# Forgetting attention: probabilities times values for two heads in one step, with the matmuls alternating between the two column halves of the TensorE array

## What is computed

```python
H_ATT = 16; HEAD_DIM = 64; Q_BLOCK = 128; s = 256

def forgetting_attention(q, k, v, f_logit):
    ...
    cum = jnp.cumsum(jax.nn.log_sigmoid(f_logit.astype(jnp.float32)), axis=1).transpose(0, 2, 1)
    for blk in range(s // Q_BLOCK):
        qs, qe = blk * Q_BLOCK, (blk + 1) * Q_BLOCK
        sc = jnp.einsum("bhqd,bhkd->bhqk", q[:, :, qs:qe], k[:, :, :qe]).astype(jnp.float32) * scale
        sc = sc + cum[:, :, qs:qe, None] - cum[:, :, None, :qe]
        ...
        p = jax.nn.softmax(sc, axis=-1).astype(v.dtype)
        outs.append(jnp.einsum("bhqk,bhkd->bhqd", p, v[:, :, :qe]))
```

## Time and profile before

| | us |
|---|---|
| median of 3 runs | 1188.36 (1187.55 to 1188.62) |
| the profiled execution | 1188.64 |
| its span, first to last instruction | 1186.8 |
| TensorE matmuls busy | 1161.3 (98% of the span) |
| TensorE weight loads busy | 1089.4 (92%) |
| DVE busy | 908.3 (77%) |
| ACT busy | 713.8 (60%) |
| POOL busy | 383.9 (32%) |

### The profile page before, as it was taken

How to read it: one execution, slowest core, us unless ns; L and a number is a source line. 1 busy time by engine, 2 the same in 40 slices (tenths; PEclk the granted TensorE clock), 3 DMA queues, 4 the chain that set the end, 5 groups by cost and what they waited for, 6 DMA issues and landing times.

```text
span 1186.8 us, 23771 instructions
## 1 busy us (share of the span) xinstructions
PE 1161.3 (98%) x8406; PEld 1089.4 (92%) x8406; DVE 908.3 (77%) x1365; ACT 713.8 (60%) x1142; POOL 383.9 (32%) x406
## 2 busy tenths in 40 slices
PE   8999999999999999998999999999999999999996
PEld 8999989999999999888999988888899999888886
DVE  7867897877699999557899698777666768877754
ACT  6498655654467676435745766665445546666552
POOL 3444000700545555224000135445220006554431
PEclk9999999999999999999999999999999999999999
DMA  6566433376635666652634356666765435665661
GB/s 216 178 195 212 143 111 121 124 255 191 207 107 178 184 186 180 212 187 77 182 126 146 100 168 203 181 191 205 253 198 178 144 124 176 197 187 183 210 201 69
DMA packets 56562, 204.32 MB, mean 172 GB/s; under 512 B 6688, under 2 KB 6840, under 8 KB 56368
## 3 DMA queue, kind: packets, MB, share of 16 engines
q1 hardware_dynamic: 54288, 197.35, 53.1%
q0 software_dynamic: 1632, 5.00, 1.2%
q10 hardware_dynamic: 576, 1.05, 0.2%
HBM read 202.29 MB, written 2.63 MB: 173 GB/s over the span
## 4 chain that ended last, share of the span: by engine, by line
PE 87%; DVE 9%; ACT 2%; issue 1%; DMA 1%; POOL 0%; DVEq 0%; SPq 0%; ACTq 0%; POOLq 0%
PE bank L1450 20%; PE bank L1456 14%; PE bank L1458 14%; PE bank L1457 14%; PE bank L1451 11%; DVE w_lo L734 2%; PE bank L1453 2%; PE bank L1560 2%; PE bank L1561 2%; PE bank L1562 2%; DVE h_two L764 1%; PE bank L1647 1%; DVE work L889 1%; DVE work L788 1%; PE bank L1637 1%
## 5 line engine op out<-in xcount | busy, mean ns | idle before, releaser
L734 DVE TENSOR_TENSOR w_lo<-raw,w_hi 128x1024 fp32r<-128x1024 f32 x374 | 477.4, 1284 | 133.2 <-ACT w_hi L310 128.8
L310 ACT ACTIVATE w_hi<-raw 128x1024 fp32r<-128x1024 f32 x374 | 391.6, 1052 | 133.6 <-PE bank L1458 62.5
L1456 PE MATMUL bank<-h_two,w_hi 128*128 128x256 f32 x1184 | 342.4, 289 | 11.3 <-DVE h_two L764 7.5
L1458 PE MATMUL bank<-h_two,w_lo 128*128 128x256 f32 x1184 | 335.6, 283 | 0.0
L1457 PE MATMUL bank<-h_two,w_hi 128*128 128x256 f32 x1184 | 335.6, 283 | 0.0
L1456 PEld LDWEIGHTS bank<-h_two,w_hi 128*128 128x128 f32 x1184 | 227.6, 192 | 17.9 <-issue 8.4
L1457 PEld LDWEIGHTS bank<-h_two,w_hi 128*128 128x128 f32 x1184 | 227.7, 192 | 0.3
L1458 PEld LDWEIGHTS bank<-h_two,w_lo 128*128 128x128 f32 x1184 | 227.6, 192 | 0.0
L1450 PE MATMUL bank<-h_two,w_hi 128*128 128x512 f32 x616 | 221.5, 398 | 0.9 <-DVE h_two L764 0.9
L1451 PE MATMUL bank<-h_two,w_lo 128*128 128x256 f32 x704 | 183.6, 281 | 0.0
L1450 PE MATMUL bank<-u_two,w_hi 128*128 128x512 f32 x455 | 161.4, 398 | 0.0
(11 more groups left out here) (260 smaller groups left out, 1837.6 us busy)
## 6 DMA issues: line engine op xcount, KB each, us to landing
raw<-in_stream SPq DMA_DIRECT2D x374, 512.0 KB, 4.0
bias_rows<-bias_row POOLq DMA_DIRECT2D x1, 1536.0 KB, 15.0
work<-in_x_t SPq DMA_DIRECT2D x2, 512.0 KB, 6.0
work<-in_x_t POOLq DMA_DIRECT2D x1, 1024.0 KB, 5.7
work<-bias_rows POOLq DMA_DIRECT2D x1, 1024.0 KB, 10.6
out<-work ACTq DMA_DIRECT2D x4, 256.0 KB, 2.5
work<-bias_rows POOLq DMA_DIRECT2D x1, 512.0 KB, 5.8
work<-in_lmask POOLq DMA_DIRECT2D x1, 384.0 KB, 6.3
```

The lines of the kernel that those rows point to most:

```text
L310: A(w_hi[:, slot, :], raw[:, slot, :], ACT.Copy).then_inc(hi_ready, 1)
L734: v.tensor_tensor(w_lo[:, slot, :], raw[:, slot, :], w_hi[:, slot, :].bitcast(F32), ALU.subtract).then_inc(lo_ready, 1)
L1456: mm(out, w_hi[:, slot, s], r_two[:, 0, :], start=start, stop=False)
L1458: return mm(out, w_lo[:, slot, s], r_two[:, 0, :], start=False, stop=stop)
```

## The change

`fox_values` now takes a pair of heads, t = 0 to 7, and is called in the even turns 6 to 20 instead of a head in each of the turns 5 to 20. It waits once for both heads' copies (`pt_copied`), and then issues the same six matmuls of the pair, each of the three products for the even head and then for the odd one. One increment of 2 stands at the end of the pair. The work of an odd head stays in its turn; that of an even head moves one turn later.

```diff
-            def fox_values(h):
-                if h >= 2 and h % 2 == 0:
-                    pe.wait_ge(y_lo, h // 2)
-                o = h % 2 * DH_FOX
-                values(h, bank[7][o:o + DH_FOX, 0:S],
-                       lambda kb: flat(V[:, 4 * kb:4 * kb + 4, :])[:, h * DH_FOX:(h + 1) * DH_FOX])
+            def fox_values(t):
+
+                pe.wait_ge(pt_copied, 2 * t + 2)
+                if t >= 1:
+                    pe.wait_ge(y_lo, t)
+
+                def part(q, kb, pk, start, stop):
+                    for h in (2 * t, 2 * t + 1):
+                        o = h % 2 * DH_FOX
+                        vt = flat(V[:, 4 * kb:4 * kb + 4, :])[:, h * DH_FOX:(h + 1) * DH_FOX]
+                        last = mm(bank[7][o:o + DH_FOX, q * P:(q + 1) * P], vt, att_pt[:, h % 2, pk * P:(pk + 1) * P],
+                                  start=start, stop=stop)
+                    return last
+                part(0, 0, 0, True, True)
+                part(1, 0, 1, True, False)
+                part(1, 1, 2, False, True).then_inc(pv_mm, 2)
...
-                if 0 <= s - 5 < H_FOX:
-                    fox_values(s - 5)
+                if 0 <= s - 5 < H_FOX and s % 2 == 0:
+                    fox_values((s - 6) // 2)
```

## The result

| | before | after |
|---|---|---|
| median | 1188.36 (1187.55 to 1188.71, 5 runs) | 1181.83 (1181.41 to 1182.08, 5 runs) |
| ratio, 95% interval | | 0.9946 [0.9935, 0.9957] |
| profiled execution's span | 1186.8 | 1180.3 |

The account below looks back on a forecast made before the run. TensorE was taken as the bound, DVE close behind. Seven pairs saving 0.32 + 0.45 us each make 5.4, less 0.3 for one wait: 5.1 us, median 1188.36 to 1183.3 us; 8 in 10 range 1181.8 to 1187.0.

Parts of the forecast that it names:

- The bound and the path to the end: TensorE sets the pace; only savings before tile 19 ends, seven pairs in turns 6 to 18, reach the end.
- The 0.32 us of a call: First block's values calls: 0.32 us each is a pause from changing between 128 and 64 columns; saved once per pair.
- the first rival: The halves don't overlap; only the changes of columns are saved: 1.9 us, 1186.4 us; chance 27%.
- The overlap: Within a pair, 5 borders where the half changes save 0.09 us each, 0.45 us a pair.
- The sum's own range: Whole change: 0.05 to 0.11 us a border, 3.7 to 5.8 us saved, 1182.6 to 1184.7 us.
- The range of 8 in 10: Median of the changed kernel: from 1181.8 us, with eight pairs counting, to 1187.0 us, past the case without overlap.
- The wait of turn 6: TensorE's scores of turn 6 wait for DVE's evacuation of tile 5: 0.3 us lost, once.
- The copies, `head_out`, `head_low` at no cost: Even heads' copies and following ACT and DVE steps come later; costed at nothing, hidden by 2 to 3 us of cover.
- No overlap: Rival: the two halves' matmuls start 0.11 us apart as now; 1.9 us saved, 1186.4 us; chance 27%.
- exposed loads: Rival: at each border a load waits for the running matmul, 0.11 us each; 1.9 us slower, 1190.3 us; chance 7%.
- drains at each border: Rival: each change of half within a pair costs 0.16 us; 3.7 us slower, 1192.1 us; chance 8%.
- That ACT or DVE takes the gain back: Rival: cover missing in early turns, TensorE runs at DVE's pace, 9.15 us a pair; 3.5 us saved, 1184.8; chance 8%.

Follow-up runs that it names:

- e3: Changed kernel, but heads 14 and 15 left one by one as before, so only the first seven pairs remain; 1181.61 us.
- e4: Kernel before, with only heads 14 and 15 made a pair, in turn 20, all other heads single; 1188.26 us.
- e5: Kernel before, one head a turn, with each head's matmuls loading its pair's 128 value columns and writing all 128 partitions; 1184.04 us.
- e2: Changed kernel, from the second pair on odd heads write partitions 0 to 63 too, so all twelve passes use one half of the array; 1185.76 us.
- e9: Changed kernel with ACT's copy of head 1 in turn 5 moved ahead of that turn's `w_hi`; 1181.80 us.
- e6: Changed kernel, from the second pair on only the first product of each head, 2 matmuls instead of 6; 1180.52 us.
- e7: Changed kernel with each pair's six matmuls issued twice, first into free columns of bank 7; 1186.12 us.
- e1: Changed kernel with a pair's matmuls grouped by head, the even head's three first, then the odd head's; 1183.92 us.
- e8: Changed kernel with each matmul of a pair split into two of 32 columns, over four quarters of the array; 1181.30 us.

## Why the prediction came out as it did

- **The bound and the path to the end: right.** TensorE's time in turns 6 to 18 counted one for one, and e3 and e4 show the seven and the none of the eighth.
- **The 0.32 us of a call: right,** shown as the price of the change of columns by e5 (0.33 a head), and by e2, where from the second pair on it alone remains. e2 saves 2.5 us, 0.64 of them by the overlap in the first pair; the 1.9 left are what the first rival forecast for no overlap.
- **The overlap: right in kind, too small in size.** The step was "I take 0.09 us a border, near the upper end, 0.45 a pair"; a pair's overlap comes out at 0.66 (1.98 - 0.32 - 1.00), and at 0.64 directly against e2. The step that failed is the one ahead of it: "If the two heads overlapped everywhere it would be 6 passes, 0.66; the passes of one half are issued in twos, so I leave this out." I took the order of issue for the order of execution. The odd head's first pass starts with the even head's first, not behind its second. 7 x 0.21 = 1.5 us, which is the whole difference between 5.1 and the 6.6 of the trace. How the array chooses the order of the passes no run shows.
- **The range: reached by luck.** The sum's own range ended at 5.8 us saved and missed the result. The range of 8 in 10 reached 1181.8, but that end stood for an eighth pair that counts (7 x 0.87 - 0.3 for seven, and 0.87 more, which makes 1181.7). e3 and e4 show that it doesn't; the overlap of 0.66 a pair took its place.
- **The wait of turn 6: right in size (0.3 forecast, 0.34 measured) partly by luck.** I named the evacuation of tile 5 and overlooked that the transposes ahead of the scores need bank 6, which became free only 0.2 us before that evacuation ended. e9 shows both waits, the second behind the first.
- **The copies, `head_out`, `head_low` at no cost: right in the time, but not for the reason given.** I had DVE catch up with TensorE by 0.23 us a pair, and the copy of an even head wait for its turn's values. With 8.70 us on both sides DVE keeps its lag to the end of the heads: in turn 12 of the changed kernel it evacuates the tile 3.4 us behind its end (before: 0.2), and no copy ever waits for a pair.
- **The margin behind it was missed.** The prediction has "What TensorE saves per pair of turns counts up to 9.70 - 8.70 = 1.00 us", and the full overlap uses 0.98 of it. I weighed only my smaller sum against it. e6 shows what the next such saving would bring: nothing in turns 10 to 16, where DVE's pace holds it.
- **The rivals.** No overlap, exposed loads and drains at each border are all excluded by the six steps of twelve passes. That ACT or DVE takes the gain back, at 9.15 us a pair of turns, is excluded by the 8.70 us of both windows.

## What to carry to other kernels

In this kernel matmuls with half the columns cost twice: going to them and back paused the array for 0.33 us, and the other half idled. Putting them together in one run saves the pauses, and letting neighbours in the list write different column groups fills the other half. They should stay interleaved, since grouping by head gives back 0.26 us of the 0.64 here. And before adding up a saving, compare the bound engine's list with the next one's, piece by piece: here the gain stopped within 0.02 us of DVE's pace.

## What the runs showed of the hardware

- Two plain float32 matmuls on the two column halves, 128 rows each, run at once: starts about 7 ns apart, the next two 0.11 us later (0.16 behind the first two of a row), sustained over 24 passes (e7). The Trainium skill (TensorE: Matmul & The Clock Gate, Part 3) gives an offset of some 4 ns a tile and 2.38 times the speed for three column tiles; here two column tiles need six steps where one needs twelve, and 24 passes on four quarters take 0.79 us, no longer than 12 on two halves (0.81), with starts 7 ns apart.
- The same part of the Trainium skill says that loads overlap with running matmuls only when the row group differs. Here all rows are in use in both halves and no load is exposed, neither across the halves nor within one: in e2 a pass starts every 0.11 us though each load is recorded with 0.137. In these traces the rule doesn't hold.
- The passes of one matmul and of its neighbour in the other half start together and go on side by side. Grouped by head, a matmul of the other half starts 0.27 us behind the first, ahead of one that stands before it in the list (e1).
- Going from 128 to 64 columns and back costs 0.32 to 0.34 us, with 6 steps between (before, changed kernel) or 12 (e2, e7), and as much with 32 columns (e8); with 128 columns throughout it is gone (e5).
